# One mixing matrix for both directions of the state space stage, with the step sizes applied to C times B by ScalarE and GpSimd

## The chip, the core and the metric

The kernel runs on one core of a Trainium2 chip. The metric is the device time of one execution in microseconds (us), lower is better. The engines of the core are TensorE (PE in the profile; PEld is its weight load), VectorE (DVE), ScalarE (ACT), GpSimd (POOL) and SyncE (SP), which issues the DMAs.

## What is computed

The program is two transformer-like blocks on 512 tokens of width 1024. The change lies in one stage of the first block, a state space layer that runs over the tokens in both directions. The part of the reference that the change rewrites is this, called once with the inputs as they are and once with them flipped in time:

```python
def ssd_chunked(x, dt, A, Bm, Cm):
    ...
    xdt = (x * dt[..., None]).reshape(b, c, CHUNK, G, r, P)
    ...
    CB = jnp.einsum('bclgn,bcsgn->bcgls', Cc, Bc)
    Wd = CB[:, :, :, None] * segsum_exp(adt)
    y_diag = jnp.einsum('bcgrls,bcsgrp->bclgrp', Wd, xdt)
    ...
    y_off = jnp.einsum('bclgn,bcgrpn,bcgrl->bclgrp', Cc, prev, jnp.exp(a_cs))
    return (y_diag + y_off).reshape(b, l, H, P)
...
    y_fwd = ssd_chunked(xs, dt[:, :, 0], A[0], Bm, Cm)
    y_bwd = fl(ssd_chunked(fl(xs), fl(dt[:, :, 1]), A[1], fl(Bm), fl(Cm)))
    y = y_fwd + y_bwd + d_skip.astype(f32)[:, None] * xs
```

There are 8 groups of heads (G) with 4 heads each (r), 4 chunks of 128 tokens (c), and 64 features per head (P). C times B is shared by the heads of a group; the decays `segsum_exp` and the step sizes `dt` are one per head and direction. The forward direction fills the triangle at and below the diagonal of a chunk's 128x128 matrix, the backward direction the triangle at and above it.

## The kernel before

The program is written by hand as one instruction stream per engine, with semaphores between them; nothing reorders it. The state space stage is `ssd_sync`, `ssd_tensor`, `ssd_scalar`, `ssd_vector` and `ssd_pool`. Each goes through the 8 groups, with the front of group g+1 woven into the back of group g; the middle groups are a hardware loop.

Names used below, for group g and chunk c (c = 0 to 3):

- **features(n)** (n = 0 to 3): TensorE makes the stage's inputs of the *next* group, 24 matmuls of 128x512 each in three passes (L168 to L170). ScalarE copies the result out (`copy_up`), VectorE convolves it (`conv(n)`, L1628 and four times L1631). The weights come as a rounded high part from ScalarE (`weights_hi`) and a rest from VectorE (`weights_lo`, L1618); features(n) waits for its rest.
- **front**: three turns to token order (L1426), the z product (`z_product`), C times B, then the chunk states (L1445). VectorE multiplies C times B by the two triangle masks (`masks`, L1639, semaphore `cb_read`) and chains the states (`states`, L1650 to L1659).
- **steps** (`steps(g, n)`, L1743, n = 2c + direction): GpSimd makes the log decays of one chunk and direction, two instructions of 128x512. **sums** (L1398, L1399): TensorE adds them up. **decay** (L1539): ScalarE takes the exponential. **mixers** (L1667): VectorE multiplies it by the masked C times B.
- **weighted** (L1751): GpSimd multiplies the tokens `xt` by `dt` (two sets) and by the weights of the chunk states (two sets), four instructions of 128x256 a set. **xd** (L1766): GpSimd's d_skip times the tokens, signalled by `diag_done`.
- **y products** (L1471): TensorE multiplies each mixing matrix by the weighted tokens, forward and backward added in one PSUM tile; VectorE adds the rest (L1683 to L1696, called **y(c)** below).
- **norm** (L1702, L681 to L689, L1706): the group's normalization, on VectorE with one root on ScalarE.

VectorE's order inside the back of a group is: mixers of chunk 0, mixers of chunk 1, y(0), conv(0), weights_lo(2), mixers of chunk 2, y(1), conv(1), weights_lo(3), mixers of chunk 3, y(2), conv(2), weights_lo(4), conv(3), y(3), then norm, masks, two weights_lo, states. `mixers(g, n)` does one direction. GpSimd's order is `group(g)`: weighted for the states, steps 0 and 1, weighted by dt, steps 2 and 3, xd, steps 4 to 7. Steps n wait until TensorE has read steps n-2 (`diff_ready`), since there are two buffers `am`.

## Time and profile before

| | before |
|---|---|
| median of 3 runs (lowest, highest) | 2546.34 us (2543.79, 2547.43) |
| the profiled execution: device time | 2541.76 us |
| its span in the trace | 2539.3 us |
| TensorE, VectorE, ScalarE, GpSimd busy | 92%, 58%, 40%, 21% of the span |
| mean granted TensorE clock | 0.948 |

The stage with the change is the stretch from about 331 to 866 us of the span, a fifth of it. The shares above are averages over stages with different limits, so they say little about this one; the rows below are from its own stretch. "Idle before <-X" in a row is how long the engine stood idle before the instruction, and X what ended that. The granted clock is 1.00 at 2.4 GHz and 0.50 at 1.2 GHz.

### The profile page before, as it was taken

The page shows a single profiled execution, that of the slowest core. Times are in us where ns is not written, and L with a number is a line of the kernel's source. Part 1 is how long each engine was busy: PE and PEld are TensorE (multiplying, and loading weights), DVE is VectorE, ACT ScalarE, POOL GpSimd, SP SyncE. Part 2 cuts the span into 40 slices and gives each one's busy share as a digit, 9 for nine tenths or more (in the row PEclk, how much of TensorE's full clock was granted, in tenths as well). Part 3 has the DMA queues.
Part 4 walks back from the last instruction along what each step waited for, and adds up shares of the span by engine and source line. Part 5 has one row for each costly group of instructions (what it writes and reads, how often), then busy time and mean ns, then how long its engine had stood idle before and what let it go on. Part 6 is the DMA issues. An engine that isn't in the chain of part 4 may idle for free.

```text
span 2539.3 us, 33243 instructions
## 1 busy us (share of the span) xinstructions
PE 2326.7 (92%) x12329; PEld 1944.3 (77%) x12329; DVE 1484.1 (58%) x2230; ACT 1003.6 (40%) x1607; POOL 542.8 (21%) x618
## 2 busy tenths in 40 slices
PE   7999989999999799989999999999987997969997
PEld 6887767887888587868888878997767996757774
DVE  3555456888888754363334344566756555456665
ACT  3354523444444432343223232455333335145553
POOL 1000004555565300000000000392244440012101
PEclk8999999999999899888999999999999998979999
DMA  5310221112211333122332231422000005249995
GB/s 185 100 59 9 68 83 50 50 50 61 69 51 50 155 111 100 49 84 67 100 100 92 91 114 37 133 84 75 26 17 1 1 1 222 78 194 367 418 414 196
DMA packets 166300, 267.49 MB, mean 105 GB/s; under 512 B 9033, under 2 KB 140441, under 8 KB 156313
## 3 DMA queue, kind: packets, MB, share of 16 engines
q1 hardware_dynamic: 161705, 249.45, 28.2%
q0 software_dynamic: 4464, 16.25, 1.7%
q8 instruction: 86, 1.41, 0.2%
q14 instruction: 45, 0.37, 0.0%
HBM read 237.38 MB, written 28.31 MB: 105 GB/s over the span
## 4 chain that ended last, share of the span: by engine, by line
PE 69%; DVE 13%; DVEq 6%; ACT 5%; issue 4%; POOL 1%; DMA 1%; POOLq 1%; ACTq 0%; SPq 0%
PE ps L168 16%; PE ps L169 16%; PE ps L170 16%; PE ps L3419 3%; DVE arena L1631 2%; PE ps L596 1%; PE ps L993 1%; PE ps L2841 1%; ACT pair L354 1%; PE ps L2856 1%; PE ps L1015 1%; PE ps L1471 1%; DVEq L1657 1%; DVE arena L1667 1%; PE ps L3383 1%
## 5 line engine op out<-in xcount | busy, mean ns | idle before, releaser
L170 PE MATMUL ps<-pair,pair 128*128 128x512 f32 (+1 forms) x2248 | 824.5, 367 | 0.0
L168 PE MATMUL ps<-pair,pair 128*128 128x512 f32 (+1 forms) x1992 | 749.8, 376 | 38.2 <-DVE pair L383 14.2
L169 PE MATMUL ps<-pair,pair 128*128 128x512 f32 (+1 forms) x1992 | 752.2, 378 | 0.0
L170 PEld LDWEIGHTS ps<-pair,pair 128*128 128x128 f32 x2248 | 434.4, 193 | 71.4
L168 PEld LDWEIGHTS ps<-pair,pair 128*128 128x128 f32 x1992 | 385.0, 193 | 103.4 <-issue 40.8
L169 PEld LDWEIGHTS ps<-pair,pair 128*128 128x128 f32 x1992 | 387.5, 195 | 70.9 <-issue 6.9
L354 ACT ACTIVATE pair<-ring 128x2048 fp32r<-128x2048 f32 x102 | 194.7, 1909 | 293.9 <-PE ps L170 288.3
L360 DVE TENSOR_TENSOR pair<-ring,pair 128x2048 fp32r<-128x2048 f32 x95 | 219.0, 2306 | 143.8 <-ACT pair L354 143.8
L1751 POOL TENSOR_TENSOR arena<-arena 128x256 f32<-128x256 f32 x128 | 91.7, 749 | 502.1 <-ACT arena L1528 502.1
L1743 POOL TENSOR_TENSOR pair<-arena,pair 128x512 fp32r<-128x512 f32 x128 | 155.3, 1241 | 58.5 <-PE ps L1399 58.4
L2117 POOL MEMSET arena<- 128x1 f32 x32 | 1.0, 98 | 662.0 <-DVEq L157 661.8
L846 DVE TENSOR_TENSOR arena<-ps,arena 128x512 f32<-128x512 f32 x56 | 38.7, 690 | 151.7 <-PE ps L170 151.7
L168 PE MATMUL ps<-pair,ring_rounded 128*128 128x512 f32 x256 | 108.9, 425 | 7.1 <-DVE ring_rounded L1618 7.0
L168 PE MATMUL ps<-part,pair 128*128 128x512 f32 x256 | 103.2, 403 | 10.7 <-DVE part L402 6.1
L1631 DVE SCALAR_TENSOR_TENSOR arena<-arena 128x512 f32<-128x512 f32 x128 | 97.7, 763 | 18.6 <-issue 16.2
L169 PE MATMUL ps<-part,pair 128*128 128x512 f32 x256 | 102.3, 400 | 0.0
L170 PE MATMUL ps<-part,pair 128*128 128x512 f32 x256 | 102.1, 399 | 0.0
L1510 ACT ACTIVATE arena<-ps 128x512 f32<-128x512 f32 x32 | 19.2, 599 | 190.9 <-PE ps L170 190.9
L3705 DVE TENSOR_TENSOR pair<-ring,pair 128x2048 fp32r<-128x2048 f32 x32 | 71.9, 2288 | 25.6 <-ACT pair L3472 25.5
L2789 POOL TENSOR_TENSOR ring<-ring,arena 128x512 f32<-128x512 f32 x48 | 65.7, 1376 | 93.5 <-PE ps L2841 87.3
L3419 PE MATMUL ps<-arena 128*128 128x512 f32 x184 | 82.9, 593 | 0.5 <-ACT arena L3513 0.5
L1667 DVE TENSOR_TENSOR arena<-arena 128x512 f32<-128x512 f32 x64 | 72.5, 1181 | 16.6 <-ACT arena L1539 12.9
(516 smaller groups left out, 3906.7 us busy)
## 6 DMA issues: line engine op xcount, KB each, us to landing
ring<-in_w_in SPq DMA_DIRECT2D x54, 1024.0 KB, 6.5
arena<-in_w_exp_down SPq DMA_DIRECT2D x23, 1024.0 KB, 10.5
ring<-in_w_up SPq DMA_DIRECT2D x16, 1024.0 KB, 5.6
ring<-in_w_down SPq DMA_DIRECT2D x16, 1024.0 KB, 5.1
ring<-in_w_exp_gate SPq DMA_DIRECT2D x16, 1024.0 KB, 8.5
ring<-in_w_exp_up SPq DMA_DIRECT2D x16, 1024.0 KB, 10.6
expert_results<-arena SPq DMA_DIRECT2D x22, 512.0 KB, 11.0
ring<-in_w_in SPq DMA_DIRECT2D x16, 512.0 KB, 5.8
```

Of the source, the lines that this page charges most:

```text
L168: nc.tensor.matmul(out, lhs[1], rhs[0], start=start, stop=False)
L169: nc.tensor.matmul(out, lhs[0], rhs[1], start=False, stop=False)
L170: return nc.tensor.matmul(out, lhs[0], rhs[0], start=False, stop=stop)
L354: act.activation(self.pair.hi[:, self.home(k), 0:n], self.raw(k)[:, 0:n], ACT.Copy).then_inc(core.hi_made, 1)
L360: eng.tensor_tensor(self.pair.lo[:, self.home(k), 0:n], self.raw(k)[:, 0:n], self.pair.hi[:, self.home(k), 0:n].bitcast(F32), ALU.subtract ...
L1631: ins = dve.scalar_tensor_tensor(out=cv[:, j, :], in0=up[:, j, k:k + T], scalar=chunk(cw[:, k, :], m), in1=cv[:, j, :], op0=ALU.mult, op1= ...
L1667: dve.tensor_tensor(heads(M[:, n % 4, :]), heads(ex[:, n % 2, :]), cb[:, d, c, :].unsqueeze(1).to_broadcast([P, GH, P]), ALU.mult)\
L1743: ins = gp.tensor_tensor(out.rearrange("p a (r l) -> p (a r) l", r=GH), (LE, GE)[d].unsqueeze(1).to_broadcast([P, GH, P]), table[:, d, c, ...
L1751: ins = gp.tensor_tensor(heads(xw[:, n, c, :]), heads(xt[:, c, :]), per_head(t, g, n % 2, c), ALU.mult)
L2789: gp.tensor_tensor(NL[h], NTr[c % 2][h], over(levelsT[:, l, :]), ALU.mult).then_inc(lmasked, 1)
L3419: mm = nc.tensor.matmul(ps[:, 5 + half, :], actT[i % 2][:, k, :], w[:, k, half * 512:(half + 1) * 512], start=k == 0, stop=k == 1)
L3705: dve.tensor_tensor(wP[i % 2].lo[:, :, j * DE:(j + 1) * DE], up_raw[n].rearrange("p (k n) -> p k n", k=DC), wP[i % 2].hi[:, :, j * DE:(j + ...
```

## The change

Forward and backward sums of a chunk now go into the same PSUM tile, so there is one exponential, one mixing matrix and one y product per chunk and head instead of two. This needs the step sizes dt on C times B rather than on the tokens, since they differ by direction. ScalarE puts the forward ones on, four activations of 128x128 a chunk (`forward_steps`); GpSimd multiplies by the backward ones and adds the two (`both_steps`, two instructions of 128x512 with a drain ahead of each), into a new tile `stepped`. The tokens weighted by dt are no longer made. `xw` has two sets instead of four, and the mixing matrices `M` lie in its place.

```diff
-            xw = core.take(4, NT, GW)
+            xw = core.take(2, NT, GW)
+            stepped = core.take(NT, GH * P)
...
-                    after(pe, ex_ready, g * 8 + (n - 1))
-                    mask = (strict.hi, strict.lo)[n % 2][:, 0, :]
-                    nc.tensor.matmul(ps[:, SUMS[n % 2], :], mask, am[n % 2].lo[:, 0, :], start=True, stop=False)
...
+                    for d, mask in enumerate((strict.hi, strict.lo)):
+                        pe.wait_ge(am_ready, g * 12 + (3 * c + d + 1))
+                        nc.tensor.matmul(ps[:, SUMS[c % 2], :], mask[:, 0, :], am[d].lo[:, 0, :], start=d == 0, stop=False)
+                        mm = nc.tensor.matmul(ps[:, SUMS[c % 2], :], mask[:, 0, :], am[d].hi[:, 0, :], start=False, stop=d == 1)
+                    mm.then_inc(diff_ready, 1)
...
                         for r in range(GH):
-                            for d in range(2):
-                                mm = nc.tensor.matmul(ps[:, 7, r * 64:(r + 1) * 64],
-                                                      M[:, (2 * c + d) % 4, r * P:(r + 1) * P],
-                                                      xw[:, d, c, r * 64:(r + 1) * 64], start=d == 0, stop=d == 1)
+                            mm = nc.tensor.matmul(ps[:, 7, r * 64:(r + 1) * 64], M[:, c, r * P:(r + 1) * P],
+                                                  xt[:, c, r * 64:(r + 1) * 64], start=True, stop=True)
...
+                def forward_steps(g, c):
+                    act.wait_ge(cb_read, g + 1)
+                    for r in range(GH):
+                        ins = act.activation(stepped[:, c, r * P:(r + 1) * P], cb[:, 0, c, :], ACT.Copy,
+                                             scale=step_of(g, 0, c, r))
+                    ins.then_inc(forward_stepped, 1)
...
                         if c + 1 < NT:
-                            decay(g, 2 * c + 2)
-                            decay(g, 2 * c + 3)
+                            if c + 2 < NT:
+                                forward_steps(g, c + 2)
+                            decay(g, c + 1)
...
                     silu_z(g + 1)
+                    forward_steps(g + 1, 0)
+                    forward_steps(g + 1, 1)
                     store_y(g)
                     decay(g + 1, 0)
-                    decay(g + 1, 1)
...
-                def mixers(g, n):
+                def mixers(g, c):
+                    dve.wait_ge(am_ready, g * 12 + (3 * c + 3))
+                    dve.wait_ge(ex_ready, g * 4 + (c + 1))
+                    dve.tensor_tensor(M[:, c, :], ex[:, c % 2, :], stepped[:, c, :], ALU.mult).then_inc(m_ready, 1)
...
+                def both_steps(g, c):
+                    gp.drain()
+                    gp.wait_ge(forward_stepped, g * 4 + (c + 1))
+                    gp.tensor_tensor(heads(backward), cb[:, 1, c, :].unsqueeze(1).to_broadcast([P, GH, P]),
+                                     dt[:, 1, c, columns(g * GH, GH)].unsqueeze(2).to_broadcast([P, GH, P]), ALU.mult)
+                    gp.drain()
+                    gp.tensor_tensor(stepped[:, c, :], stepped[:, c, :], backward, ALU.add).then_inc(am_ready, 1)
...
-                    weighted(g, 0, dt)
-                    weighted(g, 1, dt)
-                    for n in range(2, 4):
-                        steps(g, n)
+                        if n % 2:
+                            both_steps(g, n // 2)
```

Also, `after(pe, y_stored, g * 2)` now stands behind the sums of chunk 0 instead of between the two directions; steps of direction 0 alone wait for `diff_ready`, now for both sums of the chunk before; and the square's scratch tile `junk` is single.

GpSimd's queue, from the steps of chunk 1 to the end of a group, before (L1743 is steps, L1766 is xd; the semaphore named is `diff_ready`):

```order
L1743 TENSOR_TENSOR pair_57<-arena,pair_53 128x512 [waits ssd_sums_ready_then_expert_rows_hi_made]
L1743 TENSOR_TENSOR pair_57<-arena,pair_53 128x512
L1743 TENSOR_TENSOR pair_58<-arena,pair_53 128x512 [waits ssd_sums_ready_then_expert_rows_hi_made]
L1743 TENSOR_TENSOR pair_58<-arena,pair_53 128x512
L1766 TENSOR_TENSOR arena<-arena 128x256 x4
L1743 TENSOR_TENSOR pair_57<-arena,pair_53 128x512 [waits ssd_sums_ready_then_expert_rows_hi_made]
L1743 TENSOR_TENSOR pair_57<-arena,pair_53 128x512
L1743 TENSOR_TENSOR pair_58<-arena,pair_53 128x512 [waits ssd_sums_ready_then_expert_rows_hi_made]
L1743 TENSOR_TENSOR pair_58<-arena,pair_53 128x512
```

The same place in the changed kernel (there L1749 is steps, L1758 and L1761 are the multiplication and the addition of `both_steps`, L1778 is xd):

```order
L1749 TENSOR_TENSOR pair_57<-arena,pair_53 128x512 [waits ssd_sums_ready_then_expert_rows_hi_made]
L1749 TENSOR_TENSOR pair_57<-arena,pair_53 128x512
L1749 TENSOR_TENSOR pair_58<-arena,pair_53 128x512 x2
L1758 TENSOR_TENSOR arena<-arena 128x512 [waits ssd_forward_steps_applied]
L1761 TENSOR_TENSOR arena<-arena 128x512
L1778 TENSOR_TENSOR arena<-arena 128x256 x4
L1749 TENSOR_TENSOR pair_57<-arena,pair_53 128x512 [waits ssd_sums_ready_then_expert_rows_hi_made]
L1749 TENSOR_TENSOR pair_57<-arena,pair_53 128x512
L1749 TENSOR_TENSOR pair_58<-arena,pair_53 128x512 x2
L1758 TENSOR_TENSOR arena<-arena 128x512 [waits ssd_forward_steps_applied]
L1761 TENSOR_TENSOR arena<-arena 128x512
```

Two instructions have come in behind the steps of every chunk, the first of them behind a wait for ScalarE, and xd and all later steps stand behind those.

ScalarE's queue behind the z product's four activations, ahead of the loop, before (L1501 is weights_hi, L1539 decay):

```order
L1533 ACTIVATE ring<-ps 128x256 [waits ssd_z_ready_then_expert_rows_normed] x4
L1501 ACTIVATE pair_55<-ring 128x1024 [waits ssd_xbc_weights_landed]
L1501 ACTIVATE pair_55<-ring 128x1024
L1539 ACT_TABLE_LOAD
L1539 ACTIVATE arena<-ps 128x512 [waits ssd_sums_ready_then_expert_rows_hi_made] x2
```

And in the changed kernel (L1534 is the z product's, L1546 `forward_steps`, L1541 decay; the semaphore of L1546 is `cb_read`):

```order
L1534 ACTIVATE ring<-ps 128x256 [waits ssd_z_ready_then_expert_rows_normed] x4
L1502 ACTIVATE pair_55<-ring 128x1024 [waits ssd_xbc_weights_landed]
L1502 ACTIVATE pair_55<-ring 128x1024
L1546 ACTIVATE arena<-arena 128x128 [waits ssd_cb_read_then_expert_weights_split]
L1546 ACTIVATE arena<-arena 128x128 x3
L1546 ACTIVATE arena<-arena 128x128 [waits ssd_cb_read_then_expert_weights_split]
L1546 ACTIVATE arena<-arena 128x128 x3
L1541 ACT_TABLE_LOAD
L1541 ACTIVATE arena<-ps 128x512 [waits ssd_sums_ready_then_expert_rows_hi_made]
```

Eight activations that wait for VectorE's masks now stand ahead of the first exponential, of which one has gone.

## Rows read from the trace of the kernel before

**Rows 1.** Windows: busy us of PE, PEld, DVE, ACT, POOL; granted clock; DMA share; GB/s

```profile
540.50:601.70 61.20, 56.63 (x325) 49.75 (x325) 51.42 (x76) 26.17 (x44) 33.77 (x37) 0.94 0.17 51
...
540.50:548.00 7.50, 7.50 (x27) 6.51 (x28) 6.44 (x10) 0.56 (x1) 3.72 (x3) 0.55 0.00 0
```

**Rows 2.** Timeline, TensorE: first y products of groups 0, 2, 3, 5, 6 and 7

```profile
419.68 2.00 PE L1471 MATMUL ps<-arena 128*128 128x64 f32 x16 [1.98 <-DVE arena L1667]
...
540.48 2.99 PE L1471 MATMUL ps<-arena 128*128 128x64 f32 x16 [1.92 <-DVE arena L1667]
...
601.69 2.79 PE L1471 MATMUL ps<-arena 128*128 128x64 f32 x16 [1.92 <-DVE arena L1667]
...
722.78 2.00 PE L1471 MATMUL ps<-arena 128*128 128x64 f32 x16 [1.90 <-DVE arena L1667]
...
782.02 2.25 PE L1471 MATMUL ps<-arena 128*128 128x64 f32 x16 [1.90 <-DVE arena L1667]
...
840.83 3.68 PE L1471 MATMUL ps<-arena 128*128 128x64 f32 x16 [0.57 <-DVE arena L1667]
```

**Rows 3.** Timeline, VectorE, one group (538 to 600) and a later one (720 to 739)

```profile
538.24 5.09 DVE L1667 TENSOR_TENSOR arena<-arena 128x512 f32<-128x512 f32 x4 [0.59 <-issue]
...
546.05 0.75 DVE L1631 SCALAR_TENSOR_TENSOR arena<-arena 128x512 f32<-128x512 f32 x1 [0.17 <-issue]
...
553.36 2.58 DVE L1667 TENSOR_TENSOR arena<-arena 128x512 f32<-128x512 f32 x2 [2.66 <-ACT arena L1539]
...
558.37 0.48 DVE L1628 TENSOR_SCALAR arena<-arena 128x512 f32<-128x512 f32 x1
...
563.58 1.28 DVE L1667 TENSOR_TENSOR arena<-arena 128x512 f32<-128x512 f32 x2
...
588.13 1.27 DVE L1639 TENSOR_TENSOR arena<-ps,arena 128x512 f32<-128x512 f32 x2
...
720.51 5.11 DVE L1667 TENSOR_TENSOR arena<-arena 128x512 f32<-128x512 f32 x4 [0.57 <-issue]
...
738.69 0.48 DVE L1628 TENSOR_SCALAR arena<-arena 128x512 f32<-128x512 f32 x1
```

**Rows 4.** Timeline, GpSimd, the end of one group's queue

```profile
585.59 5.79 POOL L1751 TENSOR_TENSOR arena<-arena 128x256 f32<-128x256 f32 x8
592.59 4.40 POOL L1743 TENSOR_TENSOR pair<-arena,pair 128x512 fp32r<-128x512 f32 x4 [1.22 <-PE ps L1399]
596.95 2.69 POOL L1766 TENSOR_TENSOR arena<-arena 128x256 f32<-128x256 f32 x4
599.60 5.82 POOL L1743 TENSOR_TENSOR pair<-arena,pair 128x512 fp32r<-128x512 f32 x4
```

**Rows 5.** Single lines: count, then duration min/median/max in ns, first and last start

```profile
L1667 DVE TENSOR_TENSOR arena<-arena x46: 681/1522/1529, 477.1 to 794.4; 128x512 f32<-128x512 f32 x46
...
L1743 POOL TENSOR_TENSOR pair<-arena,pair x96: 1032/1216/2016, 459.1 to 795.3; 128x512 fp32r<-128x512 f32 x96
...
L2789 POOL TENSOR_TENSOR ring<-ring,arena x48: 1260/1272/1714, 1917.7 to 2090.2; 128x512 f32<-128x512 f32 x48
```

**Rows 6.** ScalarE: groups by shape, then the timeline of one exponential

```profile
L2230 ACT ACTIVATE arena<-arena 128x128 f32<-128x128 f32 x2 | 0.5, 302 | 0.0
...
600.22 0.60 ACT L1539 ACTIVATE arena<-ps 128x512 f32<-128x512 f32 x1 [0.23 <-DVE arena L1667]
```

**Rows 7.** Timeline, TensorE: y products of chunk 2, and the turn of y

```profile
562.02 1.89 PE L1471 MATMUL ps<-arena 128*128 128x64 f32 x16
...
588.26 1.10 PE L1407 MATMUL ps<-arena,ring 128*128 128x128 f32 x8 [1.09 <-DVE ring L1706]
```

**Rows 8.** Timeline, the last group: GpSimd's last steps and VectorE's last mixers

```profile
840.18 10.63 POOL L1743 TENSOR_TENSOR pair<-arena,pair 128x512 fp32r<-128x512 f32 x8
...
852.85 1.28 DVE L1667 TENSOR_TENSOR arena<-arena 128x512 f32<-128x512 f32 x2
```

More of the change, by code:

```diff
@@ L1445, in front @@
                             mm = nc.tensor.matmul(ps[:, n // 2, (n % 2) * GW:(n % 2 + 1) * GW], Bt[:, c, :],
-                                                  xw[:, 2 + d, c, :], start=True, stop=True)
+                                                  xw[:, d, c, :], start=True, stop=True)
                             n += 1
@@ L1449, in front @@
                     sums(g, 0)
-                    sums(g, 1)
+                    after(pe, y_stored, g * 2)
                 def back(g, between):
@@ L1455, in back @@
                         if c + 1 < NT:
-                            sums(g, 2 * c + 2)
-                            sums(g, 2 * c + 3)
+                            sums(g, c + 1)
                         t = slice(c * P, (c + 1) * P)
@@ L1771, in group @@
                         steps(g, n)
+                        if n % 2:
+                            both_steps(g, n // 2)
                 group(0)
```

69 lines of the change are left out of this document (31 added, 38 removed).

## The prediction

> **What bounds the kernel now.** The page puts TensorE at 92% of the whole span, but the stage of the change is to be read by itself. I first set the groups' starts beside each other: the first y products of groups 0, 2, 3, 5, 6 and 7 [rows 2]. From the first to the last are 421.15 us for seven periods; one is 61.21 us, another 59.24. Then the windows of one period [rows 1]: TensorE is busy 56.6 of 61.2 us and VectorE 51.4, and at the period's start TensorE is granted 0.55 of its clock for 7.5 us, behind a wait of 1.9 us [rows 1, 2]. TensorE starts every group's y products only when VectorE has made the mixers, so VectorE's chain sets the start of a period [rows 2]. The timeline of VectorE shows it: in the slow period there is one real gap, 2.66 us ahead of chunk 2's mixers, in which it waits for ScalarE's exponential and so for TensorE; from there to the next group's mixers it works on [rows 3]. In the quick period the stretch from the first mixers to conv(1) takes 18.18 us (720.51 to 738.69) against 20.13 (538.24 to 558.37): the gap has closed, and what is left is VectorE's own time [rows 3]. So VectorE is what the stage can't go below, and TensorE loses to it and now and then pays with its clock.
>
> The third thing to see is that VectorE's durations are not its own. A pair of mixers takes 1.28 us when GpSimd is idle, 0.60 from one to the next, and 2.58 when it is not; four take 5.1 [rows 3]. The one line has durations of 681 ns and of 1522 [rows 5]. GpSimd's steps, 1.03 us at the least, take 5.82 us for four beside those mixers, 1.45 each [rows 4, 5]. So the two take turns: where both want SBUF, one instruction of each costs 1.45 us. That adds 0.85 us to a mixer (1.45 less 0.60) and, if a convolution instruction takes its turn in the same way, 0.53 to it (1.45 less the 0.92 = 0.75 + 0.17 from one to the next [rows 3]). No row shows the convolution beside steps; this is my estimate from the mixers.
>
> **The change, part by part, for a middle group.** I count from the end of VectorE's masks, 589.40 in the timeline (588.13 + 1.27) [rows 3].
>
> *TensorE.* Half of the y products go: 1.89 us for 16 becomes 0.95 for 8, four times a group, so 3.8 us of TensorE's time [rows 7]. The sums are the same number. As VectorE sets the pace I count this at nothing; what hides it is the wait ahead of the y products.
>
> *VectorE.* Before: eight mixers, 5.09 + 2.58 + 1.28 = 8.95 us [rows 3]. After: four, 0.60 each if alone, 2.4.
>
> *ScalarE.* Four exponentials of 0.60 us go and sixteen activations of 128x128 come, 0.302 us each and about 0.25 one behind another [rows 6]: from 2.4 to 4 us. ScalarE has room (26.2 us busy of 61.2 [rows 1]). But the copies stand in the queue where something waits for them: chunk 0's can't start before the masks end, so `stepped` has its forward part at +1.1; four more stand ahead of the exponential of chunk 1. That one now starts 0.8 us after the first mixers (600.22, against 538.24 + 61.2 = 599.44 [rows 3, 6]) and moves 1 us back.
>
> *GpSimd.* Eight instructions of 128x256 go (5.79 us [rows 4]) and eight of 128x512 come. Their price no row shows. From below the steps' least, 1.03; from above, for the addition, whose two inputs are whole tiles, a GpSimd addition of that shape elsewhere, 1.26 [rows 5]. I take 1.03 alone and 1.45 in turns for both, since one of the two is built like a step. Removed work lay at 585.6 to 591.4, beside norm and masks; the new work can't stand there, since it waits for ScalarE, and GpSimd idles instead. Both parts of chunk 0 run from +1.1 to +4.3 (beside weights_lo), steps of chunk 1 to +8.7 (4.40 as before [rows 4]), its both_steps to +11.5, xd to +14.1 (2.69 [rows 4]). Before, xd ended at +10.2 (596.95 + 2.69). So diag_done, for which y(0) waits, is 3.9 us later. From +14.1 there are steps of chunk 2, both_steps, steps of chunk 3, both_steps: twelve instructions. Before there were eight there, of which four fell beside mixers that waited anyway.
>
> *The sum on VectorE.* It begins the mixers of chunk 0 at +10.3 (before +10.04, the 0.3 for a weights_lo that takes one more turn) and ends them at +11.5 behind one turn. The exponential of chunk 1 allows the next at +12.4; it ends at +13.0. y(0) waits for xd until +14.1. Now the twelve GpSimd instructions alternate with y(0), conv(0), weights_lo(2), mixers of chunk 2 and most of y(1). Twelve turns of 1.45 are 17.4 us, to +31.5, and the end of y(1) puts the start of conv(1) at +32.3. (The same work alone is 20.13 - 5.09 - 2.66 - 2.58 + 0.60 = 10.4 us, so I charge 18.2 - 10.4 = 7.8 us for twelve, 0.65 each, between the 0.53 and the 0.85 from above.) That is 22.0 us after the first mixers. In the slow period it was 20.13, so +1.9; in the quick one 18.18, so +3.8 [rows 3]. Behind conv(1) GpSimd is idle and all is as before, except that TensorE's features(3), which wait for weights_lo(3) right behind conv(1), are late by the same. TensorE had 1.09 us of waiting for norm in front of the turn of y [rows 7], which takes that much of it up. So a slow period gets 0.3 + 1.9 - 1.1 = 1.1 us longer, a quick one 0.3 + 3.8 - 1.1 = 3.0: both come to 62.25 us. Seven are 435.75, against 421.15: **+14.6 us**.
>
> *The last group* has nothing to weave in. There GpSimd's eight last steps take 10.63 us from 840.18, and the last mixers end at 852.85 + 1.28 = 854.1 [rows 8]. Now xd ends about 843.2 and twelve instructions follow, mostly alone: eight steps at 1.15 and four at 1.2 make 14, to 857.3, a mixer more makes 858.1: **+4 us**. The first group I leave at nothing, since its VectorE has no convolution before it and the same order.
>
> Total +18.6 us on the profiled execution's 2541.8. The runs' median is 2546.3, 4.6 above it, so 2565 us.
>
> **A rule against the rows.** In the turns above a convolution or a mixer delays GpSimd by 0.42 (1.45 less 1.03), not by its whole 0.68, so rows say that the turns overlap a little [rows 4, 5]. The Trainium skill, "SBUF — State Buffer", section "Who interferes with whom", says that a VectorE instruction with two SBUF inputs and a GpSimd instruction that reads SBUF exclude each other, and that the second one "fully blocks" until the first is done. The trace agrees that they exclude each other; the length is shorter than that.
>
> **The rivals.**
> (1) *Each turn costs its full length.* If each of the twelve instructions holds VectorE for its whole 1.03 us where I have counted 0.65, the period grows by another 12 x 0.38 = 4.6, and the sum by 32 us: 2597. This is what that page's rule would give here. The additions at 1.26 instead of 1.03 go the same way with 2 x 0.23 a period, +3 us, and a period in which the longer waits of TensorE bring the 0.55 clock [rows 1] loses up to 2 us more (61.21 less 59.24 [rows 2]), +14. Against it: rows 3 to 5. Together 14%.
> (2) *Faster: GpSimd's instructions fall into VectorE's pauses.* Each convolution instruction has a drain of 0.17 us behind it, and a GpSimd instruction that gets in there costs less than I count. At half my price, 0.33 us for each of twelve, the period is 3.9 us shorter, 58.35, and TensorE, which has shed 3.8 us, doesn't stop it: 7 x 58.35 = 408.5, so -12.7 + 4 = -9 us, 2537. It decides from 18.6 / 84 = 0.22 less than mine, 0.43 us an instruction: below that the seven periods and the tail together gain. For it: 6.5 us of mixers are removed for certain. Against it: the order moves GpSimd's work out from beside the mixers to beside the convolution. 24%.
> (3) *No difference.* VectorE's saving and the turns cancel. The price lies near 0.43 us, or xd and the exponential are not waited for (2.0 us a period of my sum, 14 us in all). 2546, 17%.
>
> **How the numbers follow.** My forecast has 45%: 2565, its own range 2552 to 2580. Rival (1) 14%, (2) 24%, (3) 17%. About 0.2%, 5 us, is what a measurement of this kernel can tell from no change. Faster is (2), 0.24; same is (3) with nothing of the forecast, 0.17; slower is the rest, 0.59. The range leaves out a tenth at each end: 2535, a little below (2)'s own time, to 2588, between the forecast's upper end and (1)'s 2597.
>
> **What would show it.** In the changed trace: period of the first y products near 62 us in all middle groups, without quick ones; VectorE idle ahead of y(0) about 1 us, released by GpSimd's xd; convolution instructions of conv(0) near 1.3 us instead of 0.75, beside steps; GpSimd idle some 3 to 5 us between steps of chunk 0 and its both_steps, released by ScalarE; norm quicker by about 1.3 us. I am wrong if conv(0) keeps its 0.75 us a piece, if TensorE's granted clock moves the periods more than VectorE does, or if the new GpSimd instructions take much more or less than 1.0 to 1.3 us.

## The result, and the profile after

| | before | changed |
|---|---|---|
| median of the runs on the same chip | 2545.07 us (4 runs) | 2570.16 us (2568.22 to 2578.02, 4 runs) |
| ratio, 95% interval | | 1.0126 [1.0108, 1.0144] |
| span in the trace | 2539.3 us | 2568.3 us |
| mean granted TensorE clock | 0.948 | 0.939 |

The changed kernel is slower by 25 us; 2565 was predicted. In the changed kernel L1677 is the mixers, L1643 and L1640 the convolution, L1630 weights_lo, L1662 to L1671 states, L1692 to L1702 the y of a chunk, L1712 the last scaling of norm; on GpSimd L1749 is steps, L1758 and L1761 the multiplication and the addition of `both_steps`, L1778 xd; on ScalarE L1541 is decay and L1546 `forward_steps`. The page's first part, busy time by engine:

```profile
PE 2312.6 (90%) x12073; PEld 1926.5 (75%) x12073; DVE 1485.0 (58%) x2198; ACT 1025.0 (40%) x1703; POOL 576.8 (22%) x618
```

VectorE is busy 1485.0 us over the whole span, where the page of the kernel before has 1484.1: what it shed in mixers it gained elsewhere, and only the stage's own windows tell where. First all seven periods of the kernel before, from the first y products of group 0 to those of group 7 [rows 2] (window and its length, busy us of TensorE, its weight loads, VectorE, ScalarE and GpSimd, the granted clock, the share of DMA and its GB/s):

```profile
419.68:840.83 421.15, 387.09 (x2245) 340.05 (x2245) 359.26 (x524) 179.89 (x297) 234.89 (x252) 0.95 0.18 53
```

The same view of the changed kernel: all seven, then a short and a long period as the y products' starts cut them, and pieces of both.

```profile
423.12:863.62 440.50, 367.02 (x2021) 316.24 (x2022) 364.12 (x495) 197.72 (x383) 267.84 (x253) 0.93 0.17 50
...
550.50:612.32 61.82, 52.36 (x292) 45.07 (x292) 52.19 (x71) 28.12 (x54) 37.84 (x36) 0.94 0.17 51
612.32:676.71 64.39, 53.38 (x293) 46.13 (x292) 52.66 (x71) 29.26 (x58) 38.89 (x38) 0.92 0.17 49
...
565.90:575.00 9.10, 9.06 (x30) 7.27 (x31) 8.06 (x12) 1.05 (x2) 3.30 (x3) 0.74 0.00 0
...
638.00:653.00 15.00, 12.00 (x65) 10.60 (x64) 13.41 (x21) 7.56 (x14) 1.46 (x2) 0.89 0.47 133
```

Seven periods take 440.50 us against 421.15, +19.35. VectorE's busy time grew by 4.9 us of that (364.12 less 359.26); its idle time grew by 14.5, from 61.9 (421.15 less 359.26) to 76.4. The groups of instructions of VectorE in these two windows show what is inside. Before (busy us, mean ns of one | idle us ahead of them):

```profile
L1631 DVE SCALAR_TENSOR_TENSOR arena<-arena 128x512 f32<-128x512 f32 x112 | 85.6, 765 | 17.4 <-issue 16.2
L1667 DVE TENSOR_TENSOR arena<-arena 128x512 f32<-128x512 f32 x57 | 64.3, 1177 | 16.3 <-ACT arena L1539 12.9 <-issue 3.2
...
L1706 DVE TENSOR_SCALAR ring<-ring,arena 128x256 f32<-128x256 f32 x28 | 17.4, 680 | 0.5
...
L1691 DVE TENSOR_TENSOR ring<-ring,arena 128x256 f32<-128x256 f32 x21 | 9.9, 474 | 1.9
...
L1650 DVE COPY arena<-ps 128x256 f32<-128x256 f32 x14 | 5.2, 410 | 3.2 <-PE ps L1445 3.2
```

The same groups of the changed kernel:

```profile
L1643 DVE SCALAR_TENSOR_TENSOR arena<-arena 128x512 f32<-128x512 f32 x112 | 103.2, 921 | 17.4 <-issue 16.2
...
L1677 DVE TENSOR_TENSOR arena<-arena 128x512 f32<-128x512 f32 x29 | 31.2, 1075 | 18.7 <-ACT arena L1541 13.1 <-issue 2.6 <-POOL pair L1749 1.8
...
L1697 DVE TENSOR_TENSOR ring<-ring,arena 128x256 f32<-128x256 f32 x21 | 17.6, 838 | 1.9
...
L1692 DVE TENSOR_TENSOR arena<-ps,arena 128x256 f32<-128x256 f32 x21 | 8.7, 415 | 7.1 <-POOL arena L1778 7.1
...
L1712 DVE TENSOR_SCALAR ring<-ring,arena 128x256 f32<-128x256 f32 x28 | 8.0, 349 | 0.5
...
L1662 DVE COPY arena<-ps 128x256 f32<-128x256 f32 x14 | 5.3, 420 | 8.2 <-PE ps L1450 8.1
```

Over seven periods the mixers gave back 33.1 us (64.3 less 31.2) and norm's scaling 9.4, and the convolution (+17.6 here), the sums of y (+7.7 in L1697 alone) and others took it again. In the right-hand column the idle time grew ahead of y, where xd is late (7.1), and ahead of the states, where TensorE is late (8.2, before 3.2). These two don't cost the same, as the part on the prediction shows. The timeline of VectorE in the short period shows the wait for xd and the turns (start, us; the last two rows are from the last group):

```profile
548.92 1.53 DVE L1677 TENSOR_TENSOR arena<-arena 128x512 f32<-128x512 f32 x1 [0.69 <-issue]
551.87 0.74 DVE L1677 TENSOR_TENSOR arena<-arena 128x512 f32<-128x512 f32 x1 [1.42 <-ACT arena L1541]
553.23 0.42 DVE L1692 TENSOR_TENSOR arena<-ps,arena 128x256 f32<-128x256 f32 x1 [0.61 <-POOL arena L1778]
...
557.89 1.45 DVE L1643 SCALAR_TENSOR_TENSOR arena<-arena 128x512 f32<-128x512 f32 x1 [0.17 <-issue]
...
563.83 2.06 DVE L1630 TENSOR_TENSOR ring_rounded<-ring,pair 128x1024 fp32r<-128x1024 f32 x1
...
570.98 0.48 DVE L1640 TENSOR_SCALAR arena<-arena 128x512 f32<-128x512 f32 x1
571.63 0.75 DVE L1643 SCALAR_TENSOR_TENSOR arena<-arena 128x512 f32<-128x512 f32 x1 [0.17 <-issue]
...
596.43 0.92 DVE L687 TENSOR_SCALAR arena<-arena 128x4 f32<-128x4 f32 x1
597.43 0.92 DVE L689 TENSOR_TENSOR arena<-arena 128x4 f32<-128x4 f32 x1
...
610.98 1.29 DVE L1677 TENSOR_TENSOR arena<-arena 128x512 f32<-128x512 f32 x1 [0.68 <-POOL pair L1749]
...
892.30 0.17 DVE L687 TENSOR_SCALAR arena<-arena 128x4 f32<-128x4 f32 x1
892.55 0.16 DVE L689 TENSOR_TENSOR arena<-arena 128x4 f32<-128x4 f32 x1
```

From the first mixers to conv(1) it is 22.06 us (548.92 to 570.98), where 22.0 was predicted, and 40.0 more to the next group's mixers; in the long period behind it, it is 23.05 (610.98 to 634.03) and 41.1. A convolution instruction takes 1.45 us while GpSimd works and 0.75 when GpSimd has ended, as before [rows 3]. The mixers of chunk 0 take 1.53 us beside the addition of chunk 1 (GpSimd has it from 548.62 to 549.90), as a mixer did beside steps [rows 5]. GpSimd's timeline beside it, which answers to [rows 4]:

```profile
540.04 1.04 POOL L1758 TENSOR_TENSOR arena<-arena 128x512 f32<-128x512 f32 x1 [5.12 <-ACT arena L1546]
541.22 1.29 POOL L1761 TENSOR_TENSOR arena<-arena 128x512 f32<-128x512 f32 x1
...
557.76 1.04 POOL L1758 TENSOR_TENSOR arena<-arena 128x512 f32<-128x512 f32 x1 [0.31 <-issue]
558.94 1.52 POOL L1761 TENSOR_TENSOR arena<-arena 128x512 f32<-128x512 f32 x1
560.43 6.36 POOL L1749 TENSOR_TENSOR pair<-arena,pair 128x512 fp32r<-128x512 f32 x4
```

And TensorE behind it, at the features that need weights_lo(2), and at the turn of y of the last group:

```profile
565.94 0.79 PE L168 MATMUL ps<-pair,ring_rounded 128*128 128x512 f32 x1 [6.01 <-DVE ring_rounded L1630]
566.53 0.63 PE L169 MATMUL ps<-pair,pair 128*128 128x512 f32 x1
...
893.98 1.97 PE L1412 MATMUL ps<-arena,ring 128*128 128x128 f32 x8 [6.31 <-DVE ring L1712]
```

TensorE stands for 6.0 us (5.6 in the first of the seven periods) until the slowed convolution lets VectorE come to weights_lo; its matmuls then take 0.63 us, where they take 0.40 at the full clock, and the granted clock is 0.74 over 9 us. In the period from 722.8 us of the kernel before, the waits have 1.0 us for weights_lo.

The rest of the 29.0 us of span lies ahead of and behind the seven periods. Group 0's y starts 3.4 us later (423.12 less 419.68). The turn of y of the last group ends the stage. In the changed kernel it is the last row above; in TensorE's timeline of the kernel before:

```profile
864.25 1.97 PE L1407 MATMUL ps<-arena,ring 128*128 128x128 f32 x8 [6.31 <-DVE ring L1706]
```

From the last group's y products it is 23.4 us before and 30.4 after: +6.9. From there to the end of the span it is 1675.0 and 1674.3, so nothing. 3.4 + 19.35 + 6.9 - 0.7 = 29.0.

### The profile page after: what moved, and what is told of

Its sections match the earlier page's. It is cut to its first block, busy times and chain, and to the rows that moved or that the text cites. A ratio compares the mean times of both kernels' runs of the same rounds, so it can differ in the third digit from the quotient of the medians.

```text
span 2568.3 us, 32709 instructions
## 1 busy us (share of the span) xinstructions
PE 2312.6 (90%) x12073; PEld 1926.5 (75%) x12073; DVE 1485.0 (58%) x2198; ACT 1025.0 (40%) x1703; POOL 576.8 (22%) x618
## 4 chain that ended last, share of the span: by engine, by line
PE 68%; DVE 11%; ACT 5%; DVEq 5%; issue 3%; POOL 3%; POOLq 3%; DMA 1%; ACTq 0%; SPq 0%
PE ps L168 17%; PE ps L169 16%; PE ps L170 16%; PE ps L3433 3%; DVE arena L1643 2%; POOL pair L1749 1%; PE ps L596 1%; PE ps L2855 1%; PE ps L993 1%; ACT pair L354 1%; POOLq L1756 1%; PE ps L2870 1%; PE ps L1015 1%; DVEq L1642 1%; DVEq L1695 1%
## 5 line engine op out<-in xcount | busy, mean ns | idle before, releaser
L1765 POOL TENSOR_TENSOR arena<-arena 128x256 f32<-128x256 f32 x64 | 46.1, 753 | 502.9 <-ACT arena L1529 502.9
L1749 POOL TENSOR_TENSOR pair<-arena,pair 128x512 fp32r<-128x512 f32 x128 | 153.1, 1224 | 0.2
L1643 DVE SCALAR_TENSOR_TENSOR arena<-arena 128x512 f32<-128x512 f32 x128 | 115.2, 900 | 18.6 <-issue 16.2
L168 PEld LDWEIGHTS ps<-pair,ring_rounded 128*128 128x128 f32 x256 | 52.1, 204 | 68.7 <-DVE ring_rounded L1630 45.1
## 6 DMA issues: line engine op xcount, KB each, us to landing
ring<-in_w_exp_up SPq DMA_DIRECT2D x16, 1024.0 KB, 11.1
```

What stands on the lines that cost most here:

```text
L168: nc.tensor.matmul(out, lhs[1], rhs[0], start=start, stop=False)
L1643: ins = dve.scalar_tensor_tensor(out=cv[:, j, :], in0=up[:, j, k:k + T], scalar=chunk(cw[:, k, :], m), in1=cv[:, j, :], op0=ALU.mult, op1= ...
L1749: ins = gp.tensor_tensor(out.rearrange("p a (r l) -> p (a r) l", r=GH), (LE, GE)[d].unsqueeze(1).to_broadcast([P, GH, P]), table[:, d, c, ...
L1765: ins = gp.tensor_tensor(heads(xw[:, n, c, :]), heads(xt[:, c, :]), per_head(t, g, n, c), ALU.mult)
```

## The experiments

All kernels ran with several runs each beside the kernel before, and each ratio is to those. Its runs had medians of 2538.5 to 2545.1 us from one set to the next, so the ratios are compared here, and a time expected in us is read as a ratio to the 2545 from which it was reckoned. The table has, from each trace, the window from group 0's first y products to group 7's, and of it what VectorE was busy and what it was not (the length less the busy time), and TensorE's mean granted clock in it.

| kernel | ratio, interval | seven periods | VectorE busy | idle | clock |
|---|---|---|---|---|---|
| before | 1 | 421.15 | 359.26 | 61.9 | 0.95 |
| changed | 1.0126 [1.0108, 1.0144] | 440.50 | 364.12 | 76.4 | 0.93 |
| changed, once more | 1.012 [1.01, 1.014] | 442.13 | 363.60 | 78.5 | 0.93 |
| no backward steps | 0.9957 [0.9939, 0.9975] | 412.28 | 326.16 | 86.1 | 0.93 |
| multiplication thrice | 1.0224 [1.0194, 1.0253] | 462.84 | 383.86 | 79.0 | 0.91 |
| xd early | 1.0086 [1.006, 1.0112] | 435.52 | 370.83 | 64.7 | 0.92 |
| y products twice | 1.016 [1.0133, 1.0186] | 448.15 | 366.12 | 82.0 | 0.92 |
| steps on VectorE | 1.0111 [1.0087, 1.0134] | 437.79 | 373.63 | 64.2 | 0.92 |
| memsets on GpSimd | 1.0182 [1.0152, 1.0213] | 447.29 | 365.26 | 82.0 | 0.91 |
| xd and exponential early | 1.0077 [1.005, 1.0104] | 433.60 | 373.60 | 60.0 | 0.93 |
| both steps on ScalarE | 0.9968 [0.9945, 0.9991] | 409.93 | 352.72 | 57.2 | 0.98 |
| ... once more | 0.9969 [0.9954, 0.9984] | 410.01 | 352.76 | 57.3 | 0.98 |
| ... and the sum on VectorE | 1.0001 [0.999, 1.0012] | 413.82 | 359.46 | 54.4 | 0.96 |
| ... and the sum on GpSimd | 1.0032 [1.0021, 1.0044] | 420.98 | 347.96 | 73.0 | 0.94 |

Two traces of the changed kernel differ by 1.6 us in the seven periods (440.50 and 442.13); smaller differences between kernels are not read.

**Without the two instructions.** The kernel leaves the backward step sizes out of the computation; VectorE's mixers wait for ScalarE's copies themselves.

```diff
                 def both_steps(g, c):
-                    gp.drain()
                     gp.wait_ge(forward_stepped, g * 4 + (c + 1))
-                    gp.tensor_tensor(heads(backward), ...)
-                    gp.drain()
-                    gp.tensor_tensor(stepped[:, c, :], stepped[:, c, :], backward, ALU.add).then_inc(am_ready, 1)
```

> The changed kernel without the two GpSimd instructions of both_steps (so the backward step sizes are left out of the computation); GpSimd still waits for ScalarE's forward steps in the same places, and VectorE for them too. Changed kernel: about 2571 us where the kernel before has 2545. Turns (each GpSimd instruction that falls beside VectorE's work costs VectorE about 0.65 us): xd comes some 2 us earlier and five or more turns beside y(0), conv(0) and y(1) go, about 5 us a period, and the last group gains its 8 us: 2525 to 2535, faster than the kernel before. Waits alone (ScalarE's copies and the late xd cost the time, the turns nothing): only xd's earlier start and the last group gain, 2550 or more. TensorE's clock: no more than 10 us off the changed kernel.

Measured: 2525.64 us, ratio 0.9957, inside the range of the turns. The profiled execution was the slowest of ten (2540.71 us), so its trace shows less of the gain than the median. In it the periods fall by 28.2 us and VectorE's busy time by 38.0, which for 56 instructions in seven periods is 0.68 each; my price was 0.65. So what makes the changed kernel slower is GpSimd's work: with the copies and the waits for them, but without it, the kernel is faster than the one before. The copies are not free, though. VectorE's idle time is 86.1 us here, the highest of the table; 24.3 of it are ahead of the mixers, for an exponential that stands behind copies in ScalarE's queue, and 15.4 ahead of the states, for TensorE. With so little to do VectorE is no longer what holds the period alone, which is why 38.0 us less work gave back 28.2.

**Two more multiplications in chunks 2 and 3.**

```diff
-                    gp.tensor_tensor(heads(backward), ..., ALU.mult)
+                    for _ in range(3 if c >= 2 else 1):
+                        if _:
+                            gp.drain()
+                        gp.tensor_tensor(heads(backward), ..., ALU.mult)
```

> The changed kernel with the backward multiplication made three times over in chunks 2 and 3, a drain between: four GpSimd instructions of 128x512 more a group, all in the stretch beside y(0), conv(0) and y(1), for which nothing waits there but mixers of chunks 2 and 3. Turns at 0.65 us each: 2.6 us a period more and 4 to 5 us in the last group, about +20 us over the changed kernel, 2591. If each costs its whole length, 1.04 us and its drain, +35 us, 2606. Waits alone: VectorE waits at most for the addition of chunk 2, below +8 us.

Measured: 2595.13 us, ratio 1.0224; 22.3 us more in the periods for 28 instructions, 0.80 each. VectorE's busy time grew by 19.7, 0.70 each. By the ratios that is 25 us over the changed kernel, between the +20 of the turns and the +35 of full lengths, and nearer to the turns. The rows decide more sharply than the time: 0.70 us of VectorE's time an instruction is far from 1.04.

**Memsets in their place.** Four memsets stand where two multiplications stood. They need the same time on GpSimd, but read nothing.

```diff
                     gp.drain()
+                    for _ in range(4 if c >= 2 else 0):
+                        gp.memset(backward, 0.0)
+                        gp.drain()
                     gp.wait_ge(forward_stepped, g * 4 + (c + 1))
```

> The changed kernel with four memsets of 128x512 and a drain behind each on GpSimd ahead of the backward multiplication of chunks 2 and 3. They read nothing from SBUF and only write. The kernel with two more multiplications there, which read, lost 25 us to the changed one, 3.2 us a period for four instructions. If the price is that of the turns at SBUF, which I took from instructions that read, write-only work costs little: 0 to +10 us over the changed kernel. If the price is the length of GpSimd's queue (the later steps of chunk 3), or writing takes turns as reading does, the loss is in proportion to the added GpSimd time, +15 us or more.

Measured: ratio 1.0182, some 14 us over the changed kernel by the ratios, 9 by the two spans (2577.7 and 2568.3). This is above the +10 us that the turns alone allowed and just under the 15 for the length of the queue, so the time alone doesn't decide between them; its interval overlaps with that of the multiplications. The rows of the two traces do. GpSimd in seven periods, memsets:

```profile
L1758 POOL MEMSET arena<- 128x512 f32 x56 | 30.7, 549 | 6.8
```

VectorE beside the four memsets that start at 560.64:

```profile
560.95 0.75 DVE L1643 SCALAR_TENSOR_TENSOR arena<-arena 128x512 f32<-128x512 f32 x1 [0.17 <-issue]
561.88 0.75 DVE L1643 SCALAR_TENSOR_TENSOR arena<-arena 128x512 f32<-128x512 f32 x1 [0.17 <-issue]
```

And in the kernel with the multiplications, beside its three that start at 564.09:

```profile
564.23 1.45 DVE L1643 SCALAR_TENSOR_TENSOR arena<-arena 128x512 f32<-128x512 f32 x1 [0.17 <-issue]
565.85 1.28 DVE L1643 SCALAR_TENSOR_TENSOR arena<-arena 128x512 f32<-128x512 f32 x1 [0.17 <-issue]
```

Memsets take no turns: VectorE's convolution keeps its 0.75 us beside them, and VectorE's busy time grew by 1.1 us in all. The multiplications added 30.8 us to GpSimd (L1761 62.7 against 31.9 of its line in the changed kernel), the memsets 30.7; the periods grew by 22.3 and by 6.8. So of 0.80 us an instruction, by these two traces, 0.55 is the turns and 0.24 the longer queue. The second part reaches VectorE by way of TensorE and ScalarE: ahead of the z product ScalarE stands 30.0 us in the seven periods for TensorE (17.4 in the changed kernel), its copies come behind that, and from the end of the masks to the end of xd it is 15.5 to 16.9 us in the middle groups (15.4 to 15.8), in the mean 0.8 more, as much as a period got longer. The Trainium skill, "SBUF — State Buffer", section "Who interferes with whom", says that a VectorE instruction with two SBUF inputs contends with a GpSimd instruction that reads SBUF and not with one that only writes it; the trace agrees (1.28 to 1.50 us beside the one, 0.75 beside the other). The words "fully blocks", which the prediction takes from there, stand on the page with VectorE's two-port modes; for two inputs it says that they contend, under a rule of an exclusive lock.

**xd ahead of chunk 0's `both_steps`.**

```diff
-                    for n in range(4):
+                    for n in range(2):
                         steps(g, n)
-                        if n % 2:
-                            both_steps(g, n // 2)
+                    after(gp, y_read, g * 4)
+                    for c in range(NT):
+                        ins = gp.tensor_tensor(heads(xd[:, c, :]), heads(xt[:, c, :]), ...)
+                    ins.then_inc(diag_done, 1)
+                    both_steps(g, 0)
+                    for n in range(2, 4):
+                        steps(g, n)
+                    both_steps(g, 1)
```

> The changed kernel with GpSimd's xd moved ahead of both_steps of chunk 0, into the 4 to 5 us in which GpSimd waits for ScalarE. Same work. Both the turns and the waits expect a gain: y(0) no longer waits for xd but only for the exponential and TensorE (1 to 2 us), and all of GpSimd's later instructions come 2.7 us earlier, so two or so of them fall beside the wait ahead of y(0) instead of beside conv(1): 1.5 to 2.5 us a period and 2.7 in the last group, 2551 to 2558. If what counts is TensorE alone, no change from 2571.

Measured: 2559.71 us, ratio 1.0086. That is a gain, but a smaller one than expected: 2551 to 2558 is 1.0023 to 1.0051, and by the ratios some 10 us came back where 13 to 20 were expected. The periods are 5.0 us shorter and the last group takes 28.0 us instead of 30.4 (856.28 to 884.27). VectorE's idle time fell by 11.7 us and its busy time rose by 6.7: more than half of a wait that goes comes back as turns, above all in norm's scalings, which take 17.4 us in the periods where they took 8.0.

**The exponential ahead of the copies, on top of it.**

```diff
-                            if c + 2 < NT:
-                                forward_steps(g, c + 2)
                             decay(g, c + 1)
+                            if c + 2 < NT:
+                                forward_steps(g, c + 2)
```

> The kernel with xd ahead of chunk 0's both_steps, which ran at 1.0086 of the kernel before, and besides in ScalarE's queue the exponential of chunk c+1 ahead of the forward copies of chunk c+2, where the changed kernel has it behind. In the trace of the changed kernel the second mixers wait 1.42 us for the exponential, behind 1.27 us of copies. If VectorE's waits count, a period gets 0.7 to 1.4 us shorter: 5 to 10 us, 1.005 to 1.007. If the turns fill the time anyway, GpSimd's twelve instructions run on and the time stays: 1.0075 to 1.009.

Measured: ratio 1.0077 [1.005, 1.0104], in the second range, with an interval that covers both, and not to be told from the kernel with xd early. In the traces the periods are 1.9 us shorter, idle less 4.7, busy more 2.8: 0.3 us a period, hardly more than two traces of one kernel differ by.

**y products twice.**

```diff
-                            mm = nc.tensor.matmul(ps[:, 7, r * 64:(r + 1) * 64], M[:, c, r * P:(r + 1) * P], ...)
+                            for _ in range(2):
+                                mm = nc.tensor.matmul(ps[:, 7, r * 64:(r + 1) * 64], M[:, c, r * P:(r + 1) * P], ...)
```

> The changed kernel with every y product made twice into the same place (TensorE's saving undone, everything else as it is). If VectorE sets the pace, as predicted, no more than 0 to +4 us over 2571: only y(0)'s and y(3)'s products could be waited for. If TensorE sets it, 3.8 us a group, +25 to +30 us.

Measured: ratio 1.016, by the ratios 9 us over the changed kernel, though the two intervals just touch; between the 0 to +4 of "VectorE alone" and the +25 of "TensorE". It is 7.65 us in the periods for 29.7 us more of TensorE's time (396.73 busy against 367.02). So TensorE's work counts with about a quarter of itself, not with nothing. VectorE is busy 2.0 us more and idle 5.6 more. Here too ScalarE stands longer for TensorE ahead of the z product (25.0 us, 17.4 in the changed kernel), and its copies with it.

**The backward steps on VectorE.**

```diff
+                    for r in range(GH):
+                        part = stepped[:, c, r * P:(r + 1) * P]
+                        dve.scalar_tensor_tensor(out=part, in0=cb[:, 1, c, :], scalar=step_of(g, 1, c, r), in1=part,
+                                                 op0=ALU.mult, op1=ALU.add)
+                    dve.drain()
```

> VectorE does the backward steps itself: four scalar_tensor_tensor of 128x128 a chunk ahead of its mixer (C times B by the step, plus the forward part), and GpSimd's two instructions of both_steps go. Nothing is left out. A period gets 16 VectorE instructions more than in the kernel without both_steps, which ran 12.8 us under the kernel before; a drain comes with each chunk. By the turns, GpSimd's eight instructions cost VectorE some 4 us a period (that kernel's seven periods were 412.3 us against 440.5) and the sixteen cost it an estimated 0.25 to 0.35 us each, 4 to 5.6, so the time comes to that of the changed kernel or up to 15 us below it: 1.003 to 1.013 of the kernel before. If what costs in the changed kernel is only the waits for ScalarE's copies, which stay, this kernel is slower than the changed one by the whole of the sixteen, some 30 us: over 1.02.

Measured: ratio 1.0111, inside the range and as the changed kernel. Against the kernel without backward steps VectorE is busy 47.5 us more for 112 instructions, 0.42 each where I had estimated 0.25 to 0.35: these take turns too. In its trace four take 1.13 us alone and 3.48 beside GpSimd's steps. Work that GpSimd sheds to VectorE is paid in full.

**Both directions' steps on ScalarE.** 32 copies a group, two mixers a chunk from one exponential, both directions added up by TensorE in the y products; GpSimd has neither `both_steps` nor the tokens times dt. ScalarE makes an exponential ahead of the copies.

```diff
+                    for d in range(2):
+                        for r in range(GH):
+                            ins = act.activation(stepped[:, 2 * (c % 2) + d, r * P:(r + 1) * P], cb[:, d, c, :], ACT.Copy,
+                                                 scale=step_of(g, d, c, r))
...
+                    for d in range(2):
+                        dve.tensor_tensor(M[:, (2 * c + d) % 4, :], ex[:, c % 2, :], stepped[:, 2 * (c % 2) + d, :],
+                                          ALU.mult).then_inc(m_ready, 1)
```

> ScalarE puts both directions' steps on (32 copies of 128x128 a group instead of 16), GpSimd has no both_steps and no other work in its place, VectorE makes two mixers a chunk from one exponential, and TensorE adds both directions up in the y products, as before the change. Against the kernel before, GpSimd's eight instructions for the tokens times step and four exponentials go. By the turns VectorE has 6.5 us a period more than the changed kernel in mixers, but meets eight GpSimd instructions fewer (some 0.65 us each, 5.2), and has ScalarE's exponential ahead of the copies: near the kernel before, 0.993 to 1.004. If ScalarE's copies are what paces (0.31 us each, 10 us a group, four ahead of nearly every exponential), it is slower than 1.008.

> The kernel in which ScalarE puts both directions' steps on, once more with more runs, since its interval (0.9945 to 0.9991) came near to no difference: 0.9950 to 0.9985 if it is faster than the kernel before, an interval around 1 if it is not.

Measured: 2531.69 us, ratio 0.9968 [0.9945, 0.9991], and with more runs 2532.53, 0.9969 [0.9954, 0.9984]. It is faster than both kernels, though only 0.3% faster than the one before. A middle period of it:

```profile
598.83:656.80 57.97, 53.87 (x325) 47.20 (x325) 50.51 (x75) 33.32 (x72) 29.42 (x29) 1.00 0.18 54
```

58.0 us, four times in a row, with the whole clock granted. ScalarE is busy 33.3 of 58.0 us with its 32 copies (224 of them, 68.4 us in the seven periods), and they don't slow VectorE: the convolution's mean is 770 ns (765 before).

**The sum on VectorE, or on GpSimd**, ahead of one mixer a chunk, with half of the y products.

```diff
+                    dve.tensor_tensor(forward, forward, backward, ALU.add)
+                    dve.drain()
                     dve.wait_ge(ex_ready, g * 4 + (c + 1))
+                    dve.tensor_tensor(M[:, c, :], ex[:, c % 2, :], forward, ALU.mult).then_inc(m_ready, 1)
```

> Everything as in the kernel in which ScalarE puts both directions' steps on (ratio 0.9968, periods of 58.0 us), but VectorE adds the two directions up (a 128x512 addition and a drain a chunk, ahead of the wait for the exponential) and makes one mixer a chunk instead of two; so TensorE has half of the y products, 3.8 us a period less. VectorE has as many 128x512 instructions as there and four drains more. If VectorE alone paces, the time is that kernel's or up to 0.7 us a period more: 0.996 to 1.000. If TensorE, busy 53.9 of 58.0 us there, shares the pace, it is faster: 0.990 to 0.995.

> As the kernel in which ScalarE puts both directions' steps on, but GpSimd adds them up, one 128x512 addition a chunk (1.28 us alone), and VectorE makes one mixer a chunk. GpSimd thus has half of the eight instructions that the change gave it, without drains. By the turns, at the measured 0.8 us for an instruction with its drain and 0.65 without, the four cost VectorE 2.6 to 3.2 us a period, and the four mixers fewer give back 2.4 to 3.4: 0.995 to 1.003. If chunk 0's addition is late (GpSimd's steps stand around it) and the mixers wait, up to 1.008.

Measured: 1.0001 [0.999, 1.0012] and 1.0032 [1.0021, 1.0044], both just over the upper end of their first ranges; the gain expected if TensorE shared the pace did not come. The first has as many 128x512 instructions on VectorE as the kernel of 0.9969 and 16.4 us less of TensorE's time in the periods, and is 8 us slower. VectorE is busy 6.7 us more, and what TensorE shed doesn't make up for it; TensorE now waits 23.0 us for weights_lo in the periods (8.4) and is granted 0.96 in place of 0.98. In the second GpSimd's four additions cost more than the four mixers that they spare: 11.1 us of periods more than with two mixers. VectorE is busy 4.8 us less there, since the convolution's turns (102.6 us, 86.2 without the additions) take back half of the mixers, and it waits 15.8 more, most of it for the exponential (14.8 us, 3.1 without).

**The changed kernel once more.**

> The changed kernel once more, beside the others on the same chip: 1.010 to 1.014.

Measured: 2570.9 us, 1.012 [1.01, 1.014].

## Why the prediction was right, and where its size was off

*GpSimd's turns cost VectorE 0.65 us an instruction.* Shown: 0.68 by leaving `both_steps` out, 0.70 by adding to it (0.80 in all), and next to nothing for work that doesn't read. The turns of the convolution, which no row of before showed, are there (1.28 to 1.50 us). Rival (1), full lengths, is out by the kernel with more multiplications; rival (2) needed 0.43.

*VectorE sets the pace.* For the greater part. 38.0 us less of its work gave back 28.2 and 29.7 us more of TensorE's cost 7.65. But from the end of the masks to y(0) it is GpSimd's queue, fed by ScalarE's copies, that sets it: VectorE waits there for the exponential and for xd.

*The signs.* VectorE waits for xd ahead of y(0) 0.61 and 1.18 us in the two periods and 7.1 in seven; GpSimd waits 5.12 and 4.12 for ScalarE ahead of two groups; norm's four scalings take 1.14 us where they took 2.48. The addition alone takes 1.29 us, not 1.03 (the mean is 1408 ns beside VectorE); this was the +3 of rival (1). "No quick periods" seems to have failed: by the starts of the y products three are 61.6 to 61.9 us and four 63.3 to 64.4. But the y products follow the first mixers, and those stand in a stretch in which VectorE waits anyway: where they come 1.3 us earlier behind the masks, the waits for the exponential and xd are longer (2.01 and 1.18 us against 1.42 and 0.61). Counted from conv(1) to conv(1), behind these waits, all six periods of the changed kernel are 62.9 to 63.2 us. The same count gives the kernel before three of 61.2 and three of 59.5 to 59.7. So the sign holds, at 63.1 instead of 62.25.

*The sum of the periods: +14.6 predicted, +19.35 measured.* To see which term was short, take the rows at the places that the sum names: VectorE's masks, y(0) and conv(1), GpSimd's `both_steps` and xd, ScalarE's copies, and two rows of ScalarE a group earlier.

```profile
599.48 1.28 DVE L1651 TENSOR_TENSOR arena<-ps,arena 128x512 f32<-128x512 f32 x2
616.27 0.42 DVE L1692 TENSOR_TENSOR arena<-ps,arena 128x256 f32<-128x256 f32 x1 [1.18 <-POOL arena L1778]
634.03 0.48 DVE L1640 TENSOR_SCALAR arena<-arena 128x512 f32<-128x512 f32 x1
...
602.45 1.76 POOL L1758 TENSOR_TENSOR arena<-arena 128x512 f32<-128x512 f32 x1 [4.12 <-ACT arena L1546]
604.35 1.47 POOL L1761 TENSOR_TENSOR arena<-arena 128x512 f32<-128x512 f32 x1
613.36 2.77 POOL L1778 TENSOR_TENSOR arena<-arena 128x256 f32<-128x256 f32 x4
...
600.99 2.46 ACT L1546 ACTIVATE arena<-arena 128x128 f32<-128x128 f32 x8 [0.54 <-DVE arena L1651]
...
538.04 0.66 ACT L1534 ACTIVATE ring<-ps 128x256 f32<-128x256 f32 x2 [3.37 <-PE ps L170]
538.59 2.44 ACT L1546 ACTIVATE arena<-arena 128x128 f32<-128x128 f32 x8
```

The middle groups, us:

| stretch | before | in the sum | changed |
|---|---|---|---|
| end of the masks to end of xd | 10.2 to 10.4 | 14.1 | 15.4 to 15.8 |
| start of y(0) to conv(1) | 13.2 to 14.9 | 18.2 | 17.7 to 17.8 |
| conv(1) to end of the masks | 31.0 to 31.1 | 29.95 | 29.6 to 29.8 |

The term that was too small is the first one, GpSimd's way to xd. The sum had both parts of chunk 0 from +1.1 to +4.3 and xd's end at +14.1. In these rows they run from +1.7 to +5.1: ScalarE's copies release them later, and they take turns with weights_lo (1.76 and 1.47 us); the steps of chunk 1 end at +9.6, its `both_steps` at +12.6 and xd at +15.4. In the group of 538 TensorE is late with the z product, ScalarE's copies start 1.2 us behind the masks instead of 0.2, and xd ends at +15.7. The twelve turns were sized 0.5 us too high (18.2 against 17.7), and "behind conv(1) all is as before" came out right by luck: the sum took 1.1 us off there for a wait of TensorE, while VectorE's rows have the 1.3 us of the quicker norm, which the sum left out.

TensorE's stand of about 6 us behind the convolution's turns, and the 0.74 of its clock after it, are in every period, and cost little in the end. The rows show two ways by which they reach VectorE. One is the late z product, worth 0.3 to 0.5 us at xd in the groups where it shows. The other is the wait ahead of the states (1.59 us in the long period behind 612.3): it falls in front of mixers that wait for the exponential and xd anyway, and the periods from conv(1) to conv(1) are the same with and without it. TensorE's granted clock is 0.92 in the long periods and 0.92 to 0.94 in the short ones; as both are 63.1 us from conv(1) to conv(1), it isn't what moves them. What the stand costs has no experiment of its own.

*TensorE's saving is worth nothing.* Nearly: doubling the y products costs a quarter of their time. Halving them in the kernel of 0.9969 came with additions on VectorE, and did not make up for these.

*The last group: +4 predicted, +6.9 measured.* xd ended 1.2 us later than in my sum (867.22, 3.6 behind the first y products, instead of 2.4), GpSimd's last twelve instructions took 14.6 us (867.22 to 881.86) instead of 14, with a gap of 0.31 us ahead of every multiplication, and the way from the last mixer to the turn of y was 1.3 us longer (882.59 to 893.98, before 854.13 [rows 8] to 864.25), since VectorE there waits for TensorE.

*The first group: 0 predicted, +3.4 measured.* 2.3 us of it were there before any changed instruction had run: GpSimd's first weighting of tokens starts at 396.64 instead of 394.35. In the other traces it is between 393.3 and 398.0. The cause of the remaining 1.1 us stays open; GpSimd waits 9.00 us for ScalarE's copies there.

*The total: 2565 predicted, 2570.16 measured.* The sum had +18.6 us; it is +25 between the medians and +29.0 between the two traces. So the mechanism and the price of a turn were right, and the range had room for a way to xd that was 1.3 to 1.7 us too short in every middle group.

## What to carry to other kernels

Ahead of moving elementwise work to an idle GpSimd, look at what VectorE does at that moment, not at GpSimd's share: each instruction that reads SBUF beside VectorE's two-input instructions cost VectorE 0.55 to 0.7 us here, while ScalarE did the same multiplications as copies with a scale and left VectorE's durations as they were. Count a period between two places behind the last wait, here from conv(1) to conv(1). Counted from the y products, periods of 63.1 us looked like quick and slow ones, and the difference was only how long VectorE waited ahead of and behind its first mixers. A stand of TensorE, 6.0 us long and with a lower clock behind it, looked like the cause and mostly wasn't. And look at the unchanged part of the span before reading a small difference: behind the stage, two executions of one kernel (both steps on ScalarE) differed by 10.5 us, 1683.2 against 1672.7.

## What the runs showed of the hardware that was not expected

GpSimd's memsets (128x512, 549 ns) left VectorE's instructions at their full speed, while GpSimd instructions that read slowed them from 0.75 to 1.28 to 1.50 us. VectorE's instructions with PSUM as one input kept 0.41 us beside a working GpSimd. Its instructions of 128x4 in norm did not: 0.92 us each beside GpSimd in the middle groups (L685 to L689), and 0.16 in the last group, where GpSimd is idle. Four rows of VectorE's timeline above show it, two at 596 and 597 us and two at 892. 0.92 us is most of the 1.03 of a step, which GpSimd was making then. The reciprocal just ahead of them (L681, 128x4) kept 0.18 us beside the same steps.
